# Expert weights in whole rows, splits of 2048 columns in three slots, one activation table in the expert loop

## The reference

```python
logits = (x2 @ w_router + b_router).astype(jnp.float32)
top_v, top_i = lax.top_k(logits, TOP_K)
gates = jax.nn.softmax(top_v, axis=-1)
...
def expert_block(args):
    xe, e = args
    gu = xe @ w_gate_up[e] + b_gate_up[e]
    gate, up = gu[:, :D_FF], gu[:, D_FF:]
    gate = jnp.minimum(gate, SWIGLU_LIMIT)
    up = jnp.clip(up, -SWIGLU_LIMIT, SWIGLU_LIMIT)
    h = gate * jax.nn.sigmoid(SWIGLU_ALPHA * gate) * (up + 1.0)
    return h @ w_down[e] + b_down[e]
...
return jnp.sum(y * gates[..., None].astype(y.dtype), axis=1)
```

## Time and profile before

| | |
|---|---|
| median of three runs | 1706.46 us |
| span of the profiled execution | 1704.3 us |
| outside that span, by the median | 2.2 us |
| TensorE busy | 1545.6 us, 91% |
| DVE busy | 1441.4 us, 85% |
| ACT busy | 1119.6 us, 66% |
| GpSimd busy | 179.1 us, 11% |
| mean granted TensorE clock | 0.956 |
| data moved by DMA | 471 MB, 276 GB/s in the mean |

### The profile page before, as it was taken

The page is one execution under the profiler, slowest core; times in us unless marked ns, Lnnn a source line. Parts: engine busy times, 40 slices in busy tenths (PEclk is TensorE's granted clock), DMA queues, the critical chain, the costliest instruction groups (busy, mean ns, idle before and its releaser), DMA issues. The chain is left out here.

```text
span 1704.3 us, 23868 instructions
## 1 busy us (share of the span) xinstructions
PE 1545.6 (91%) x7224; PEld 1211.2 (71%) x7225; DVE 1441.4 (85%) x1947; ACT 1119.6 (66%) x1262; POOL 179.1 (11%) x196
## 2 busy tenths in 40 slices
PE   5979998859999999999999999999999999999650
PEld 4868744447777777777777777777777777777530
DVE  3965557669999999999999999999999999999547
ACT  4110231148888888888888888888888888887431
POOL 5470031000000000000000000000000000000000
PEclk9979999869999999999999999999999999999785
DMA  8400073349999999999999999999999999999206
GB/s 266 59 18 12 30 282 119 114 145 323 344 354 348 358 339 341 339 349 342 343 343 344 350 341 344 349 334 338 352 348 356 346 344 342 343 334 370 87 11 260
DMA packets 202341, 471.18 MB, mean 276 GB/s; under 512 B 18081, under 2 KB 19077, under 8 KB 201775
## 3 DMA queue, kind: packets, MB, share of 16 engines
q1 hardware_dynamic: 190910, 451.31, 74.9%
q0 software_dynamic: 11232, 19.46, 3.5%
q10 hardware_dynamic: 168, 0.04, 0.0%
HBM read 463.59 MB, written 23.04 MB: 286 GB/s over the span
## 5 line engine op out<-in xcount | busy, mean ns | idle before, releaser
L1449 DVE TENSOR_TENSOR w_lo<-ring_lo,w_hi 128x1024 fp32r<-128x1024 f32 x528 | 615.0, 1220 | 57.7 <-ACT w_hi L1293 56.1
L1293 ACT ACTIVATE w_hi<-ring_lo 128x1024 fp32r<-128x1024 f32 x528 | 549.7, 1059 | 107.5 <-PE bank L1375 97.4
L1375 PE MATMUL bank<-w_hi,x_hi 128*128 128x512 f32 x1056 | 343.8, 407 | 23.7 <-DVE w_lo L1449 21.5
L1375 PE MATMUL bank<-w_lo,x_hi 128*128 128x512 f32 x1056 | 327.9, 392 | 0.0
L1375 PE MATMUL bank<-w_hi,x_lo 128*128 128x512 f32 x1056 | 327.3, 391 | 0.0
L1449 DVE TENSOR_TENSOR w_lo<-w_out,w_hi 128x1024 fp32r<-128x1024 f32 x264 | 307.9, 1218 | 0.0
L1293 ACT ACTIVATE w_hi<-w_out 128x1024 fp32r<-128x1024 f32 x264 | 277.6, 1058 | 29.0 <-PE bank L1375 28.0
L1375 PEld LDWEIGHTS bank<-w_hi,x_hi 128*128 128x128 f32 x1056 | 192.4, 190 | 74.6 <-DVE w_lo L1449 35.4
L1375 PEld LDWEIGHTS bank<-w_lo,x_hi 128*128 128x128 f32 x1056 | 199.4, 189 | 43.1
L1375 PEld LDWEIGHTS bank<-w_hi,x_lo 128*128 128x128 f32 x1056 | 199.4, 189 | 42.8
L1375 PE MATMUL bank<-w_hi,h_hi 128*128 128x512 f32 x528 | 176.5, 415 | 0.4 <-DVE h_lo L1462 0.2
(11 more groups left out here) (316 smaller groups left out, 1600.3 us busy)
## 6 DMA issues: line engine op xcount, KB each, us to landing
ring_lo<-in_w_gate_up SPq DMA_DIRECT2D x264, 1024.0 KB, 7.0
w_out<-in_w_down SPq DMA_DIRECT2D x132, 1024.0 KB, 5.7
ring_lo<-in_w_in SPq DMA_DIRECT2D x4, 2048.0 KB, 22.4
ring_lo<-expert_rows SPq DMA_DIRECT2D x4, 2048.0 KB, 14.6
w_out<-in_w_out SPq DMA_DIRECT2D x2, 2048.0 KB, 8.6
x<-in_x_prompt SPq DMA_DIRECT2D x6, 512.0 KB, 11.7
ffn_in<-hf SPq DMA_DIRECT2D x4, 512.0 KB, 2.6
out_y_p<-of_fin SPq DMA_DIRECT2D x3, 512.0 KB
```

The costliest lines, as they stand in the source:

```text
L1293: nc.scalar.activation(w_hi[:, j % SPLIT, :], unit(j), ACT.Copy).then_inc(s["w_hi"], 1)
L1375: last = nc.tensor.matmul(bank[b + u][:], v[:, k, :], w[:, j % SPLIT, u * 512:(u + 1) * 512], start=(k == 0 and first), stop=False)
L1449: v.tensor_tensor(w_lo[:, j % SPLIT, :], unit(j), w_hi[:, j % SPLIT, :].bitcast(F32), ALU.subtract).then_inc(s["w_lo"], 1)
```

## The change

Six things change together.

1. *Loads.* A weight DMA brings whole rows: gate and up in four DMAs with 16 KB a partition (both halves of two k slices), down in four with 8 KB. Before it was 2 KB and 4 KB pieces in twelve DMAs. The next expert's load goes out when the pair that last reads its place has been subtracted.
2. *Splits.* ACT and DVE work on pairs of units, 128 x 2048, in a ring of three slots: twelve pairs a body. TensorE waits once for a pair.
3. *Activation.* The sigmoid with its scale and one of the two multiplications become one activation, x * sigmoid(1.702 x), in place. Its table is loaded once before the loop.
4. *Order.* SwiGLU is placed before pairs 6 and 10 on DVE, and the activation before them on ACT too. The reading of the slots is behind pair 7. The second transposition of h is before unit 18 (before: 19). The split of the next expert's pair 0 goes ahead of the split of its tokens.
5. *Slot tables.* `slotval` holds three bf16 parts for each number, the one-hot matrix is bf16, and DVE adds the parts after `select`. `pick_row` holds one number for each expert and is broadcast when read.
6. *h.* The last operation of SwiGLU writes h permuted (a stride of 128), since the rows of `w_down` lie differently now.

```diff
-UNITS = 24
-PAIRS = UNITS // 2
+WIDE = 2 * FF
+PAIRS = 12
+LOADS = 8
+SLOTS = 3
...
-        "slotval": sb(stack, "slotval", [P, NT, E + 1, 3]),
+        "slotval": sb(stack, "slotval", [P, NT, E, 3, 3], BF16),
...
-        "pick_row": sb(stack, "pick_row", [96, E, P], BF16),
+        "pick_row": sb(stack, "pick_row", [96, E], BF16),
...
-    if j < 8:
-        half, k = j // 4, 2 * (j % 4)
-
-        src = a["w_gate_up"][0].rearrange("e (p k) (u f n) -> e f p (k u) n", p=P, u=2, f=2)[e, half, :, 2 * k:2 * k + 4]
-        dst = keep["ring_lo"][:, 2 * j:2 * j + 2, :].rearrange("p k (u n) -> p (k u) n", u=2)
+    if j < 4:
+        src = a["w_gate_up"][0].rearrange("e (p k) n -> e p k n", p=P)[e, :, 2 * j:2 * j + 2, :]
+        dst = keep["ring_lo"][:, 4 * j:4 * j + 4, :].rearrange("p (k u) n -> p k (u n)", k=2)
...
-            for j in range(PAIRS):
-                sp.wait_ge(s["w_lo"], UNITS * q + (2 * j + 2 - UNITS))
+            for j in range(LOADS):
+                sp.wait_ge(s["w_lo"], PAIRS * q + (4 + j + 1 - PAIRS))
...
             if not first:
-                act.wait_ge(s["w_used"], UNITS * q + (j + 1 - SPLIT))
-            nc.scalar.activation(w_hi[:, j % SPLIT, :], unit(j), ACT.Copy).then_inc(s["w_hi"], 1)
+                act.wait_ge(s["w_used"], PAIRS * q + (p + 1 - SLOTS))
+            nc.scalar.activation(high(p), raw(p), ACT.Copy).then_inc(s["w_hi"], 1)
...
-            nc.scalar.activation(h_sb[:, half, :], g_sb[:, half, :], ACT.Sigmoid, scale=ALPHA).then_inc(s["sig"], 1)
+            nc.scalar.activation(g_sb, g_sb, ACT.Gelu_apprx_sigmoid).then_inc(s["sig"], 1)
...
-            for j in range(SPLIT, UNITS):
-                split(q, j)
-                if j == 11:
-                    sigmoid(q, 0)
+            for p in range(SLOTS, PAIRS):
+                if p in (6, 10):
+                    gated(q, p // 10)
+                split(q, p)
...
-                if j == 19:
+                if j == 18:
                     h_transposes(q, 1)
...
-            for j in range(SPLIT, UNITS):
-                if j == 11:
-                    swiglu(q, 0)
-                elif j == 19:
-                    swiglu(q, 1)
-                elif j == 21:
-                    take_h(q, 1)
-                split(q, j)
-                if j == 11:
+            for p in range(SLOTS, PAIRS):
+                if p in (6, 10):
+                    swiglu(q, p // 10)
+                split(q, p)
+                if p == 7:
                     keep_slots(q)
                     if nxt:
                         take_slots(q + 1)
```

More of the change, by code:

```diff
@@ L924, in router @@
     mm_free = [sem("r_mm_free0"), sem("r_mm_free1")]
-    keep["landed"] = [sem(f"landed{j}") for j in range(PAIRS)]
+    keep["landed"] = [sem(f"landed{j}") for j in range(LOADS)]
     TILES = [NT - 1] + list(range(NT - 1))
@@ L933, in _ @@
         sp.dma_start(gffn[:], a["norm_ffn"].to_broadcast([P, D])).then_inc(s["gffn_in"], 16)
-        for j in range(8):
+        for j in range(4):
             weight_load(sp, a, keep, mid, 0, j).then_inc(keep["landed"][j], 16)
@@ L1101, in _ @@
         v.memset(rank[:], -1.0)
[L1102 to L1106, removed]
+        done(v.memset(slotval[:], 0.0))
+        for i in range(NT):
+            v.memset(slotval[:, i, :, 0, 0], i * P - MISS)
+            v.memset(slotval[:, i, :, 1, 0], TOPK * (i * P - MISS))
+        v.tensor_copy(slotval[:, :, :, 0, 1], tokv[:, 0:1].unsqueeze(2).to_broadcast([P, NT, E]))
+        done(v.tensor_scalar(slotval[:, :, :, 1, 1], tokv[:, 0:1].unsqueeze(2).to_broadcast([P, NT, E]), float(TOPK), None, ALU.mult))
         iota_e = tb["iota_s"][:, 0:E]
@@ L1160, in _ @@
         done(v.reciprocal(gsum[:], gsum[:]))
-        v.tensor_tensor(slotval[:, :, 0:E, 2], gate[:], gsum[:].unsqueeze(2).to_broadcast([P, NT, E]), ALU.mult)
+        done(v.tensor_tensor(gate[:], gate[:], gsum[:].unsqueeze(2).to_broadcast([P, NT, E]), ALU.mult))
+        for c in range(3):
+            part = slotval[:, :, :, 2, c]
+            done(v.tensor_copy(part, gate[:]))
+            if c < 2:
+                done(v.tensor_tensor(gate[:], gate[:], part, ALU.subtract))
         dve.wait_ge(s["rank_psum"], 1)
@@ L1333, in over @@
             take_x(b + E)
-            for j in range(SPLIT):
-                split(b + E, j)
+            for p in range(SLOTS):
+                split(b + E, p)
             body(b + E, False)
         act.sem_inc(s["y_free"], 1)
-        for j in range(SPLIT):
-            split(0, j, first=True)
+        nc.scalar.preload_act_table(ACT.Gelu_apprx_sigmoid)
+        for p in range(SLOTS):
+            split(0, p, first=True)
         take_x(0)
@@ L1365, in h_transposes @@
             for k in range(4):
-                last = nc.tensor.transpose(bank[6 + half][:, k * P:(k + 1) * P], h_sb[:, half, k * P:(k + 1) * P], ident[:])
+                last = nc.tensor.transpose(bank[6 + half][:, k * P:(k + 1) * P], h_sb[:, k * P:(k + 1) * P], ident[:])
             last.then_inc(s["hT_psum"], 1)
@@ L1386, in body @@
             pe.wait_ge(s["x_lo"], q + 1)
-            for j in range(UNITS):
+            for j in range(2 * PAIRS):
                 if j in (0, 8):
@@ L1511, in _ @@
         take_slots(0)
-        for j in range(SPLIT):
-            split(0, j)
+        for p in range(SLOTS):
+            split(0, p)
         take_x(0)
```

123 lines of the change are left out of this document (65 added, 58 removed).

## The result

The changed kernel takes 1851.91 us (1850.95 to 1853.43), the kernel before 1705.75 in the same runs: ratio 1.085, 95% interval 1.084 to 1.087, so 146 us slower. The forecast was 1848. The profiled execution has a span of 1850.0 us, 145.7 more than before.

A forecast was written before the change was run, and what follows sets the result against it. TensorE was taken as the bound, DVE close behind. Over 31 bodies, stalls less savings gave +103 us, the clock +39, the rest 0: +142 on a span of 1704.3, so 1848 us; range 1790 to 1890.

The forecast's parts named there:

- Stall A: Before the first transposition of h, TensorE waits for slots DVE reads behind pair 7: 4.2 us a body, new.
- The walk through ACT and DVE: From TensorE's load of unit 6 through splits, activation and slots on ACT and DVE: TensorE may go on at 13.06 us.
- Stall B: Before the second transposition of h, now before unit 18, TensorE waits for DVE's strided write of h: 1.18 us a body.
- The clock: TensorE's clock falls after the 4.2 us gap in each body, costing 1.25 us a body, +39 us in all.
- Transfers: Weight loads as whole rows in 16 and 8 KB packets: worth nothing, cost nothing while a body is over 34 us.
- The rival of late transfers: The gather of the next rows, behind 16 KB packets, comes late: +3 us a body, 1940 us; chance 0.07.
- with these alone: In the loop, one activation table and the shorter bf16 selection alone bring a body from 38.08 to 36.03 us.
- The router: Small pick table frees GpSimd, so TensorE's 4.74 us gap in the router goes: -4.7 us, perhaps its clock fall too.
- Sum 0: Outside the loop's bodies, gains and costs of router, first selection, last body and overflow block add to 0.
- No fall of the clock: Rival: in the loop the gap passes without lowering TensorE's clock, 1810 us; chance 0.25.
- in time and faster: Rival: in the loop DVE's wide instructions are cheap enough, a body is 36.03 us, the whole 1643 us; chance 0.07.
- cancels: Rival: in the loop the large wait is only 0.9 us with no clock fall, 1706.5 us; chance 0.03.

The follow-up runs named there:

- a1: The changed kernel with DVE keeping and reading the slots ahead of pair 6 instead of behind pair 7: 1703.3 us.
- b1: The kernel before with the slots (and the first half of h) taken behind unit 15 instead of unit 11: 1852.1 us.
- a3: The changed kernel with fifteen unused 128x512 matmuls on TensorE ahead of its wait for the indices: 1805.1 us.
- a4: The changed kernel with gate and up loaded in eight DMAs of 2 KB packets, down left at 8 KB: 1850.0 us.
- a2: The changed kernel with the selection in PSUM bank 7, so TensorE waits for the indices before the second transposition of h: 1789.8 us.
- c1: The kernel before with one activation table, the bf16 slot tables and the small pick_row; splits, order and loads unchanged: 1639.1 us.
- a6: a1 with the second transposition of h before unit 19 instead of unit 18: 1691.8 us.
- b3: The kernel before with only the bf16 slot tables, selection in five bf16 passes and the small pick_row: 1709.9 us.
- a5: a2 with gate and up loaded in 2 KB packets as in a4: 1719.7 us.
- c4: c2 with the weights loaded as whole rows again: 1651.4 us.
- c2: The changed kernel with 1024-wide splits in six slots, the order of the kernel before and a4's loads: 1649.1 us.

## Why the prediction was right

Step by step, by its own names:

- **The body, 42.65 forecast, 42.66 measured; the sum, +142 forecast, +145.7 in the span.** The mechanism was the one named: a1 removes it and b1 makes it alone.
- **Stall A, 4.2 forecast:** 4.17 in the row. The walk through ACT and DVE was right to 0.1 us, 12.98 against 13.06, with ACT's copies of 1.92 (1.91), DVE's of 2.29 (2.29), and the slots from 898.80 to 899.60 in 0.8 (0.75).
- **Stall B, 1.18 forecast:** 1.24; the strided write takes 1.09 us in the mean of 66 and not 1.02.
- **The clock, 1.25 forecast, 1.50 measured (a3), 39 against 46.8 us.** I had let part of the low stretch lie in the gap; the windows show that it begins behind it, so that work pays for all of its 3.4 us (1.6 by the step's own sum). Without the clock the body is 41.16 where 41.4 was forecast. These two errors of a quarter of a us have opposite signs, so that the body agrees to 0.01 us is luck; each term alone is off by some 8 us in the whole.
- **Transfers, nothing forecast:** a4 bears it out, with 2 us. The rival of late transfers had the gather at 11.6 us from its issue and it is 11.8; that it was hidden in the kernel after held too. That it stops being hidden as soon as Stall A is taken away by moving TensorE's wait I had not carried into the expectation of a2.
- **A body of 36.03 us "with these alone":** true of the terms, since c1 has 36.13; not of the new kernel. It would follow that without its stalls the wide kernel reaches 36, and it does not: a6 has 37.54. Stall A stood for 3.25 us of body (a3 to a1) though 4.17 were waited, and Stall B for 0.37 of 1.28. The forecast gave the wide ring a margin of 0.7 us, which any other operation of DVE eats; the waits of 0.68 and 0.67 us behind the swiglus of a6 fit that, and show once the large wait is gone. The margin itself was not measured. And the terms don't add in any order: b3 alone is worth nothing.
- **The router, -4.7 forecast: wrong.** The gap of 4.74 us was cut to 2.27, not away, as TensorE's timeline after has it:

```profile
256.62 3.67 PE L1029 MATMUL bank<-w_out,ymix 128*128 128x512 f32 x8 [2.27 <-DVEq L1135]
```

TensorE resumes 2.47 us earlier (259.09 before). GpSimd's hold on DVE did go: two of DVE's operations of ten columns, the one of the earlier trace rows among them, take 0.17 us each in place of 3.74 and 2.32, 5.72 less in all. But DVE's filling of the new table in three bf16 parts stands in the same place ahead of TensorE's wait, and it went from 2.10 us (255.28 to 257.38) to 5.35 (249.55 to 254.90); 5.72 less 3.25 is the 2.47. Two of its rows after:

```profile
250.67 1.26 DVE L1101 MEMSET slotval<- 128x1440 bf16 x1 [0.25 <-issue]
...
253.09 1.08 DVE L1105 CAST slotval<-tokv 128x160 bf16<-128x160 f32 x1
```

The forecast put all the work of the parts at the router's end (+1.5) and none here. The fall of the clock did go, as it had held possible: eight matmuls take 3.67 us, and took 5.24. By the first selection of the loop none of the gain is left (354.66 against 354.36), and it is the shorter selection that lets the first products start 1.30 us earlier. In "Sum 0" all this was 3 of 146 us.
- **No fall of the clock (0.25), in time and faster, cancels:** none came. For the faster one DVE's wide instructions would have had to run a third faster an element; they run at 1.12 ns, where the narrow ones have 1.19.

## What to carry to other kernels

When an in-order engine gets larger instructions, every small result that another engine waits for moves later by whole instructions, so first look at who waits for the short operations between them, and put those ahead of the next large one. Moving a wait away from the engine that suffers (a2) isn't the same as moving the work forward (a1): everything else that hangs on the late result stays late. A saving on one engine counts only when the engine behind it keeps up, so measure each alone and then together, as b3 and c1 show.

## What was not expected of the hardware

- One gap of 4.17 us a body lowers the clock for 3.4 us behind it, and one of 3.4 us lowers it too (b1: 0.96 in 900 to 1280). Waits of 1.0 to 2.3 us (kernel before, a1, a2) leave it at 1.00 throughout. Fifteen unused matmuls in the gap are worth 46.8 us.
- The latency of a small gather goes by how the large loads beside it are cut: 11.8 us beside whole rows and 8.1 beside pieces with wide splits (a2, a5), 10.9 and 6.2 with narrow ones (c4, c2); the kernel before has 5.8. Packet length and moment of issue were changed together. a5 and c2 have the same loads and differ by 1.9 us; GpSimd's issue, 2.17 us in a5 and 1.19 in c2, is 1.0 longer and may be part of it; the rest stays open.
- GpSimd's issue of the gather takes 2.16 us in the mean in the kernel after and 1.18 before; it is 1.19 in c2 and c4, too, which have the new tables but narrow splits. Its issue of the scatter goes the other way, 1.17 us after and 2.64 and 2.66 in c2 and c4. So the width of DVE's instructions alone does not tell it, and the cause stays open. Only in a2 and a5, where the gather is close to late, can it matter.
